# The gated-delta inverse on half columns, with the transposed copy of X made by TensorE transposes

## What is computed

```python
kb = kc * bc[..., None]
a_mat = jnp.where(strict, jnp.einsum("bnhid,bnhjd->bnhij", kb, kc) * gamma, 0.0)
lhs = a_mat + jnp.eye(c, dtype=a_mat.dtype)
rhs = jnp.concatenate([vc * bc[..., None], kb * jnp.exp(decay)[..., None]], axis=-1)
sol = lax.linalg.triangular_solve(lhs, rhs, left_side=True, lower=True, unit_diagonal=True)
u, w = sol[..., :dv], sol[..., dv:]
```

## Time and profile before

| | before |
|---|---|
| median of 3 runs | 1711.47 us (1709.11 to 1711.91) |
| the profiled execution | 1706.36 us |
| its span, first to last instruction | 1704.3 us |
| PE busy | 1629.1 us, 96% |
| DVE busy | 958.0 us, 56% |
| ACT busy | 660.8 us, 39% |
| POOL busy | 195.4 us, 11% |

### The profile page before, as it was taken

One profiled execution on the slowest core, in us unless ns is written; L12 is line 12 of the kernel. 1 busy time (PEld: TensorE's weight loads), 2 busy tenths in 40 slices (PEclk: granted clock), 3 DMA queues, 4 the chain that ended last, 5 costly groups with the idle time before them and its releaser, 6 DMA issues.

```text
span 1704.3 us, 21809 instructions
## 1 busy us (share of the span) xinstructions
PE 1629.1 (96%) x7608; PEld 1338.5 (79%) x7608; DVE 958.0 (56%) x1344; ACT 660.8 (39%) x953; POOL 195.4 (11%) x119
## 2 busy tenths in 40 slices
PE   6998899989989999999999999999999999999996
PEld 5787679768758888888878888888788888888885
DVE  4757979866466432344456667777445544444333
ACT  5333255344344321333325555454223444443221
POOL 2755656400000000000000000000000000000000
PEclk9998999999899999999999999999999999999998
DMA  7411100202112222223223332333222222222332
GB/s 286 145 63 61 55 9 1 87 1 87 63 37 87 98 98 88 98 98 99 95 69 99 93 97 89 99 90 107 92 93 99 98 88 97 98 98 79 100 92 74
DMA packets 45664, 149.49 MB, mean 88 GB/s; under 512 B 4784, under 2 KB 5936, under 8 KB 45616
## 3 DMA queue, kind: packets, MB, share of 16 engines
q1 hardware_dynamic: 42240, 139.90, 25.6%
q10 hardware_dynamic: 3376, 8.95, 1.4%
HBM read 146.47 MB, written 2.10 MB: 87 GB/s over the span
## 4 chain that ended last, share of the span: by engine, by line
PE 87%; DVE 9%; ACT 2%; DMA 1%; issue 1%; DVEq 0%; ACTq 0%; SPq 0%
PE acc L613 78%; DVE c_acc L1887 1%; DVE qkv L1815 1%; PE acc L858 1%; PE acc L880 1%; PE acc L876 1%; PE acc L944 1%; DMA raw<-panels_a 1%; PE acc L919 1%; DMA x_rows<-xN 1%; DVE tok L1844 0%; PE acc L1058 0%; PE acc L640 0%; ACT a_p L1594 0%; DVE qkv L1813 0%
## 5 line engine op out<-in xcount | busy, mean ns | idle before, releaser
L613 PE MATMUL acc<-h_hi,w_hi 128*128 128x512 f32 x1248 | 497.8, 399 | 2.9 <-DVE qkv L1815 2.1
L613 PE MATMUL acc<-h_hi,w_lo 128*128 128x512 f32 x1248 | 493.4, 395 | 0.0
L613 PE MATMUL acc<-h_lo,w_hi 128*128 128x512 f32 x1248 | 490.3, 393 | 0.0
L1765 DVE TENSOR_TENSOR w_lo<-raw,w_hi 128x1024 fp32r<-128x1024 f32 (+2 forms) x241 | 281.5, 1170 | 77.3 <-ACT w_hi L1246 55.7
L1246 ACT ACTIVATE w_hi<-raw 128x1024 fp32r<-128x1024 f32 (+2 forms) x241 | 242.4, 1009 | 181.9 <-PE acc L613 90.9
L613 PEld LDWEIGHTS acc<-h_hi,w_hi 128*128 128x128 f32 x1248 | 236.8, 190 | 55.3 <-issue 4.6
L613 PEld LDWEIGHTS acc<-h_lo,w_hi 128*128 128x128 f32 x1248 | 236.7, 190 | 53.4 <-issue 1.2
L613 PEld LDWEIGHTS acc<-h_hi,w_lo 128*128 128x128 f32 x1248 | 236.6, 190 | 52.1
L613 PE MATMUL acc<-u_hi,w_hi 128*128 128x512 f32 x256 | 100.9, 394 | 0.0
L613 PE MATMUL acc<-u_hi,w_lo 128*128 128x512 f32 x256 | 100.4, 392 | 0.0
L2158 DVE TENSOR_TENSOR x<-x,acc 128x512 f32 x32 | 22.0, 688 | 138.8 <-PE acc L613 138.3
(11 more groups left out here) (380 smaller groups left out, 2426.0 us busy)
## 6 DMA issues: line engine op xcount, KB each, us to landing
raw<-panels_a SPq DMA_DIRECT2D x112, 512.0 KB, 3.2
raw<-panels_b SPq DMA_DIRECT2D x68, 512.0 KB, 3.2
raw<-mix SPq DMA_DIRECT2D x48, 448.0 KB, 3.3
raw<-mix SPq DMA_DIRECT2D x16, 512.0 KB, 3.6
raw<-down SPq DMA_DIRECT2D x16, 384.0 KB, 3.1
raw<-down SPq DMA_DIRECT2D x16, 320.0 KB, 2.9
x<-xT ACTq DMA_DIRECT2D x4, 1024.0 KB, 11.5
x_rows<-xN ACTq DMA_DIRECT2D x2, 1024.0 KB, 10.1
```

The lines of the kernel that those rows point to most:

```text
L613: mm = e.matmul(out, w[:, w_at:w_at + wn], a, start=first and n == 0, stop=last and n == 2)
L1765: TTn(lo, raw, k.w_hi[:, ahead.slot(w)].bitcast(F32), ALU.subtract).then_inc(k.s_split_done, 1)
```

## The change

`g_x` and `g_xt` are no longer both multiplied. At a level only the half of the columns in which P can be other than zero is computed: the moving operand of the power product is the first half of each pair of blocks of g_x (64 of 128 columns, taken in runs of 2 to 32), P has 64 columns for each chunk, and so has the product for g_x. In the place of the product for g_xt comes `turn_inverse`, four transposes of the updated g_x by PE, whose changed half ACT copies into g_xt. In the last four units only g_xt is needed, as before; there the product is 64 by 64 for each chunk. DVE subtracts once per unit, on 256 columns; its three `max` and three `match_replace` now stand behind each other, each waiting for the one operation that it depends on.

```diff
+def halves(ap, lev):
+    return ap.rearrange("p (b two s) -> p two b s", two=2, s=1 << lev)
+def packed(ap, lev):
+    return ap.rearrange("p (b s) -> p b s", s=1 << lev)
...
 def power_product(u):
-            mm = e.matmul(k.ps[u % 2][:, at:at + P], k.g_b[:, b + at:b + at + P], til(k.g_x, h)[:, at:at + P],
-                          start=True, stop=True)
+            mm = e.matmul(packed(k.ps[u % 2][:, c * 64:(c + 1) * 64], lev), k.g_b[:, b + at:b + at + P],
+                          halves(til(k.g_x, h)[:, at:at + P], lev)[:, 0], start=True, stop=True)
         mm.then_inc(k.s_p_mm, 1)
+    def turn_inverse(u):
+        h = u % HEADS
+        e.wait_ge(k.s_x_done, u + 1)
+        if u >= 2:
+            e.wait_ge(k.s_xt_done, u - 1)
+        for c in range(TT):
+            at = c * P
+            mm = e.transpose(k.ps[4 + u % 2][:, at:at + P], til(k.g_x, h)[:, at:at + P], ident)
+        mm.then_inc(k.s_xt_mm, 1)
...
-        for c in range(0 if last else TT):
-            at = c * P
-            e.matmul(k.ps[2 + u % 2][:, at:at + P], til(k.g_xt, h)[:, at:at + P], k.g_p[:, b + at:b + at + P],
-                     start=True, stop=True)
-        for c in range(TT):
-            at = c * P
-            mm = e.matmul(k.ps[4 + u % 2][:, at:at + P], k.g_p[:, b + at:b + at + P], til(k.g_xt, h)[:, at:at + P],
-                          start=True, stop=True)
+        if u >= HEADS:
+            e.wait_ge(k.s_xt_done, u - HEADS + 1)
+        if last:
+            if u < UNITS - 2:
+                e.wait_ge(k.s_xt_done, u - 1)
+            for c in range(TT):
+                at = c * P
+                mm = e.matmul(k.ps[4 + u % 2][0:64, c * 64:(c + 1) * 64], k.g_p[:, b + c * 64:b + (c + 1) * 64],
+                              til(k.g_xt, h)[:, at + 64:at + P], start=True, stop=True)
+        else:
+            for c in range(TT):
+                at = c * P
+                mm = e.matmul(k.ps[2 + u % 2][:, c * 64:(c + 1) * 64], til(k.g_xt, h)[:, at:at + P],
+                              k.g_p[:, b + c * 64:b + (c + 1) * 64], start=True, stop=True)
         mm.then_inc(k.s_xp_mm, 1)
+        if 1 <= u <= UNITS - HEADS:
+            turn_inverse(u - 1)
...
 ScalarE, in unit u
-        A(til(k.g_p, u % 2), k.ps[u % 2][:], ACT.Copy).then_inc(k.s_p_copied, 1)
+        A(k.g_p[:, (u % 2) * T:(u % 2) * T + T // 2], k.ps[u % 2][:, 0:T // 2], ACT.Copy).then_inc(k.s_p_copied, 1)
...
+        if 0 <= u - 2 < UNITS - HEADS:
+            lev = 1 + (u - 2) // HEADS
+            e.wait_ge(k.s_xt_mm, u - 1)
+            A(halves(til(k.g_xt, (u - 2) % HEADS), lev)[:, 1], halves(k.ps[4 + u % 2][:], lev)[:, 1],
+              ACT.Copy).then_inc(k.s_xt_done, 1)
...
 VectorE, in unit u
-        if not last:
-            TTn(til(k.g_x, h), til(k.g_x, h), k.ps[2 + u % 2][:], ALU.subtract)
-        if rounds:
-            for qt in range(1, TT):
-                found = link(e.max(tok(TOK_M8 + 8 * qt - 8, 8), scores[qt]))
-            e.wait_ge(k.s_dve_chain, found)
-        TTn(til(k.g_xt, h), til(k.g_xt, h), k.ps[4 + u % 2][:], ALU.subtract).then_inc(k.s_x_done, 1)
+        if last:
+            own = til(k.g_xt, h)[0:64, :].rearrange("p (c t) -> p c t", c=TT)[:, :, 64:P]
+            part = k.ps[4 + u % 2][0:64, 0:T // 2].rearrange("p (c t) -> p c t", c=TT)
+        else:
+            lev = 1 + u // HEADS
+            own, part = halves(til(k.g_x, h), lev)[:, 0], packed(k.ps[2 + u % 2][:, 0:T // 2], lev)
+        TTn(own, own, part, ALU.subtract).then_inc(k.s_x_done, 1)
```

More of the change, by code:

```diff
@@ L313, in signals @@
     k.s_dve_once = sem("dve_once")
-    k.s_act_chain = sem("act_chain")
     k.s_dve_chain = sem("dve_chain")
@@ L322, in signals @@
     k.s_d_sq = sem("d_sq")
-    k.s_dq_raw = sem("dq_raw")
     k.s_qi_raw = sem("qi_raw")
@@ L371, in signals @@
     k.s_x_done = sem("x_done")
+    k.s_xt_mm = sem("xt_mm")
+    k.s_xt_done = sem("xt_done")
     k.s_wt_mm = sem("wt_mm")
@@ L1212, in scalar_program @@
     A = e.activation
-    chain = Chain(e, k.s_act_chain)
     e.wait_ge(k.s_zeroed, 1)
@@ L1419, in scalar_program @@
         A(til(k.d_relu, m), k.ps[m][:], ACT.Square).then_inc(k.s_d_sq, 1)
-        A(til(k.d_q, m), k.ps[m][:], ACT.Copy, scale=col(k, "dsa_q")).then_inc(k.s_dq_raw, 1)
+        A(til(k.d_q, m), k.ps[m][:], ACT.Copy, scale=col(k, "dsa_q"))
     for m in range(2):
@@ L2007, in vector_program @@
     assert taps.at() == CONV_TAPS
-    replaced = chain.c.at()
+    found, replaced = [0] * TT, [0] * TT
     for u in range(UNITS):
         h, last, rounds = u % HEADS, u >= UNITS - HEADS, u % 3 < 2
-        if rounds:
-            e.wait_ge(k.s_dve_chain, replaced)
         e.wait_ge(k.s_xp_mm, u + 1)
@@ L2031, in vector_program @@
             for qt in range(1, TT):
-                replaced = link(e.match_replace(scores[qt], tok(TOK_M8 + 8 * qt - 8, 8), scores[qt], TAKEN))
-    e.wait_ge(k.s_dve_chain, replaced)
+                if u:
+                    e.wait_ge(k.s_dve_chain, replaced[qt])
+                found[qt] = link(e.max(tok(TOK_M8 + 8 * qt - 8, 8), scores[qt]))
+            for qt in range(1, TT):
+                e.wait_ge(k.s_dve_chain, found[qt])
+                replaced[qt] = link(e.match_replace(scores[qt], tok(TOK_M8 + 8 * qt - 8, 8), scores[qt], TAKEN))
+    e.wait_ge(k.s_dve_chain, replaced[TT - 1])
     for qt in range(1, TT):
```

## The result

| | before | changed |
|---|---|---|
| median of 5 runs | 1711.47 us (1709.11 to 1713.15) | **1702.42 us** (1700.77 to 1703.43) |
| the profiled execution | 1706.36 us | 1700.77 us |
| its span | 1704.3 us | 1698.8 us |

The ratio is 0.9946, 95% interval 0.9932 to 0.9961: 6.7 to 11.6 us faster. Forecast was 1701.7 us. The two profiled executions differ by less than the medians, 5.6 us. So the sign and the size came out as forecast, but the trace does not add up to the forecast's 9.8 us. Most of what follows is about that.

What follows compares the result with a forecast made beforehand. PE was taken to set the loop's pace, DVE its end. 76.4 - 8.9 - 0.9 + 1.1 = 67.7 us, plus a 9.1 us tail, gave 9.8 us earlier: 1696.6 profiled, 1701.7 us median; whole range 1695.5 to 1707.5.

Steps and rivals of the forecast that it cites:

- the forecast's 9.8 us: End of the loop: the last g_xt ready at 308.1 instead of 317.9, all after it moving as a block.
- the pass is bound by its weight load: Loop products on PE: 64 moving columns cost 0.111 us a pass, as 128 do, so halving them takes nothing off.
- the transposes are the gain: PE, units 0 to 19: four transposes at 0.446 us replace the g_xt product at 0.893; together -8.9 us.
- the sum: PE's terms from loop start to the product of unit 21: 67.7 us instead of 76.4.
- The order of DVE's list: DVE in the loop: a selection round stays 3.0 us; lost overlap costs up to 0.5 us per round, hidden except in the last.
- the waits behind the keys: Four units with a transposed key: PE waits about 0.3 us each for ACT's copy of P, +1.1 us.
- the tail: Loop end, from the product of unit 21 to the last subtraction: 9.1 us, where it was 10.2.
- the new wait in front of each transpose: PE waits for the previous unit's subtraction, which DVE reaches 2 us earlier than PE asks: 0.
- the second rival: ACT or DVE slowed by short strided runs, a new wait eating part: gain 4 to 7 us, 1706.0 us; chance 0.14.
- the third rival: PE's clock falls in the loop; one 15 us stretch at the lower level gives 1716.7 us; chance 0.05.
- the three signs that the prediction named as proving it wrong: DVE waits before transposes, a clock below 1.00 between 231 and 304, or output product's start moved by under 8 us.
- The product with 64 weight columns: Units 20 to 23 on PE: 8 x 0.056 = 0.45 us instead of 0.89; -0.9 us up to unit 21, -0.9 after.

Runs made afterwards that it cites:

- turn_by_product: Changed kernel with its four transposes per unit made as plain fp32 products with the identity, two passes each; 1710.17 us, ratio to before 1.0014.
- full_first_level: Changed kernel with 128 moving columns in both products of units 0 to 3 alone, 64 from there on, ACT copying all of P there; 1697.39 us, ratio 0.9929.
- order_alone: Kernel before with only DVE's list in the changed order, products as they were; 1709.52 us, ratio 1.0006.
- half_copy_first: Changed kernel with ACT's copy of the transposed half directly behind its copy of P, ahead of the key's four operations; 1698.68 us, ratio 0.9946.
- base_again: Kernel before, unaltered, profiled a second time; its loop took 88.3 us in that execution, its runs 1708.65 us (29 runs).
- full_columns: Changed kernel with both products back on 128 moving columns and ACT copying all of P; transposes and DVE's order stay; 1699.23 us, ratio 0.9952.
- half_first_level: Changed kernel with 64 moving columns in units 0 to 3 and the last four power products, 128 between; 1702.88 us, ratio 0.9973.
- defer_round: Changed kernel with DVE's last selection round moved behind the second softening after the loop, the mask behind the third; 1699.48 us, ratio 0.9939.

## Why the prediction was right, and where not

**Right: the pass is bound by its weight load.** The forecast took 0.111 us for a pass of 64 columns with fresh weights of 128 by 128, from rows 4. Measured 0.84 / 8 = 0.105 with 64 columns and 0.89 / 8 = 0.111 with 128. Of the 0.10 us that the two products win so, the projection part gives half back, 0.75 for 0.70. The Trainium skill (TensorE: Matmul & The Clock Gate, Back-to-back issue gap) gives N / 2.4 + 2.5 ns from one isolated matmul of N columns to the next, by which 64 columns would take about half of 128; no row of any run here shows that.

**Right: the transposes are the gain.** Four in 0.45 us for a product of 0.89, and turn_by_product takes the gain away. At a clock of 1.00 in the whole loop (full_first_level) it is 67.3 us from the start to the mean, where the sum said 67.7, and 76.4 to the last subtraction, where it said 67.7 + 9.1 = 76.8.

**Right: what hides.** The order of DVE's list is worth nothing measurable (order_alone); the waits behind the keys about 1.0 for 1.1 (half_copy_first); the tail 9.06 for 9.1; the new wait in front of each transpose does not show; the strided runs of the second rival cost 0.04 us on ACT and nothing on DVE.

**Wrong: the clock.** The failed step is in the third rival, which had a chance of 0.05: "the loop had no gaps and a clock of 1.00 throughout, and the turns in it change nothing in that". The first half was read from one execution, and base_again, the same kernel, has 0.78 from 231 to 235. As for the second half, the turns indeed change nothing. But the thin passes do (or their short runs), and at one place alone: in the first units, right behind the stretch in which PE has little to do (0.98 of 3 us from 228 to 231 in the changed kernel). In all seven profiled executions with 64 columns from the first unit on, the granted clock from 235 to 239 was 0.50 to 0.75. In all seven with 128 columns there, before included, it was 1.00. I had asked only whether gaps would open, not whether the loop's own start would look different. It cost 4.7 us, half of the forecast gain; but one stretch of this kind is not the 15 us of that rival, so the sign held. Of the three signs that the prediction named as proving it wrong, two did appear: a clock below 1.00 between 231 and 304, and an output product that moved by less than 8 us, by 2.9 (378.66 to 375.72). In full_first_level, without the low stretch, it moved by 8.0 (370.65). What the Trainium skill (TensorE: Matmul & The Clock Gate, PE-mode transpose) says, that transposes do not count as work for the clock, is not borne out as the cause here: the low stretch comes without them (turn_by_product) and fails to come with all 80 (full_columns).

**Wrong: the size of one term.** The product with 64 weight columns was taken as 0.45 us, the half of 0.89; it takes 0.61 to 0.65. The forecast called 0.056 a pass the cautious end, from 16 loads in a row. The price of a load is not yet that of eight passes that something follows. Some 0.3 us in all up to unit 21.

**Right for a reason that wasn't checked: the median.** The profiled gain of 5.5 us and the 7 to 9 us of the medians do not agree. The forecast took the median of before from 5.1 us above its profiled execution and moved it by the same 9.8. In the later runs the kernel before had medians of 1707.4 to 1708.65 beside the others, and single runs from 1703 to 1716. So 1711.47 was at the high end, and the forecast's nearness, 0.7 us, is in part luck: against 1708.65 the same gain would have read 1698.9, with 1701.82 measured. The gain of the change is best put at 4.4 to 10.1 us by the larger set.

The clocks on record show what the scatter goes with. The kernel before had a clock of 0.974 to 0.981 over the whole span in its 77 later runs, and its time goes with it: the 14 runs at 0.981 have a median of 1704.2 us, the 11 at 0.975 one of 1713.0, about 1.3 to 1.5 us for each thousandth. The twelve runs of the changed kernel have 0.9758 in the mean, the 29 of the kernel before beside them 0.9783. By an estimate from these numbers, 2.5 thousandths are 3 to 4 us, and at an equal clock the two medians, 6.8 us apart, would be 10 to 11 apart. That is close to the 9.8 of the forecast, which had reckoned with no change of the clock: the mechanism gives about what was forecast, and the clock takes back some 3 to 4 us of it.

**Open: behind the loop.** From the last subtraction to the output product it was 60.7 us in before, 61.3 in full_columns and half_copy_first, 63.1 in full_first_level, 64.6 in both profiles of the changed kernel, and 67.5 in the second profile of before (base_again). It goes with the granted clock from 310 to 380: 0.95, 0.93 twice, 0.90, 0.88 twice and 0.85. Nothing there was touched. Other profiles do not divide by the width of the first units: half_first_level, with 64 columns there, had 61.3 us at 0.93, and order_alone, whose products are those of before, 62.9 at 0.90. Whether the change shifts the odds, or whether the executions of before simply lie on both sides, was not settled: one profile an experiment does not give odds.

## What to carry to other kernels

Where each pass of a product loads fresh weights, halving the moving columns buys nothing; count the passes, and prefer the form of the operation that needs fewer (a transpose of fp32 takes one where a product takes two). Look at what stands directly behind an idle stretch of TensorE: with full-width passes there the clock here stayed up or came back within some 4 us, with half-width passes at the same count it took about 7 to 10 us, though further on the two did equally well. And where runs of one kernel scatter by 5 to 10 us, a difference of two profiled executions is not the difference of the kernels; take the ledger by stage from the trace and the size from many runs, and compare their granted clocks before the times.

## What the hardware showed that I had not expected

- The low clock at the start of the loop hangs on how the moving operand of the first four units is read (64 columns, in runs of two for the power product, or 128 in one piece), at an equal number of passes in the program and with PE busy 4.00 of 4 us in both cases: in the window of 235 to 239, 17 to 20 passes at 0.50 to 0.56 (28 at 0.75 in defer_round) against 34 to 36 at 1.00. The cost was 4.7 us.
- Eight passes with 64 weight columns take 0.61 us, and the projection part behind them 0.89 instead of 0.76, although the loads of the eight stand some 0.06 us apart.
- The mask's operation of 512 columns took 2.57 us before and 2.56 us in the changed kernel, both times with POOL's panel work beside it, although the loop ended 6.8 us earlier. In defer_round, where it runs later, it took a sixth of that, 0.41 us, starting at 319.1, just after that POOL operation had ended at 318.77. That POOL's work is what slows it fits all three, but was not tested by itself. The mask's line on DVE, ns min/median/max, and the timeline row of POOL, start and us, both of defer_round:

```profile
L2060 DVE TENSOR_SCALAR d_score_b<-d_score_b x1: 414/414/414, 319.1 to 319.1; 128x512 f32<-128x512 f32 x1
```

```profile
316.42 2.35 POOL L549 TENSOR_TENSOR w_lo<-raw,w_hi 128x1024 fp32r<-128x1024 f32 x1
```
